# The compressed branch's values in three rounded products instead of one full one

## The reference, cut to what matters

```python
k_cmp = compress(kc.reshape(B, S, G, dh), pe_k, w_ck1, w_ck2)
v_cmp = compress(vc.reshape(B, S, G, dh), pe_v, w_cv1, w_cv2)
...
s_c = jnp.einsum('bqghd,bngd->bghqn', qb, k_cmp) * scale
p_c = masked_softmax(s_c, cmp_end[None, :] <= t[:, None])
o_c = jnp.einsum('bghqn,bngd->bqghd', p_c, v_cmp)
...
o = gb[..., 0:1] * o_c + gb[..., 1:2] * o_s + gb[..., 2:3] * o_w
```

## Time and profile before

| | us |
|---|---|
| three runs | 1516.87, 1518.05, 1518.22 |
| profiled execution: from its first to its last instruction (its whole time isn't listed apart) | 1515.0 |
| TensorE busy | 1499.8 (99%), 7403 matmuls |
| VectorE busy | 895.7 (59%) |
| ScalarE busy | 774.9 (51%) |
| GpSimd busy | 740.0 (49%) |
| the eight full products of the compressed values, 16 records | 8.9 |

### The profile page before, as it was taken

The page is one execution under the profiler, slowest core; times in us unless marked ns, Lnnn a source line. Parts: engine busy times, 40 slices in busy tenths (PEclk is TensorE's granted clock), DMA queues, the critical chain, the costliest instruction groups (busy, mean ns, idle before and its releaser), DMA issues.

```text
span 1515.0 us, 19796 instructions
## 1 busy us (share of the span) xinstructions
PE 1499.8 (99%) x7403; PEld 1185.8 (78%) x7403; DVE 895.7 (59%) x1435; ACT 774.9 (51%) x1237; POOL 740.0 (49%) x462
## 2 busy tenths in 40 slices
PE   9999999999999999999999999999999999999997
PEld 7776657888888888888887787777888888888885
DVE  5568994242235764947545623532102699999998
ACT  6578885223344323132344644632224588888885
POOL 4456675445584745565464664743557362141100
PEclk9999999999999999999999999999999999999999
DMA  9210002322243564555222331121226389999984
GB/s 374 76 51 2 15 15 107 110 91 90 98 139 120 202 222 167 208 188 195 91 90 70 118 118 56 56 84 59 96 99 254 121 344 411 405 394 383 390 336 179
DMA packets 74942, 250.87 MB, mean 166 GB/s; under 512 B 11712, under 2 KB 13056, under 8 KB 74840
## 3 DMA queue, kind: packets, MB, share of 16 engines
q1 hardware_dynamic: 67264, 234.41, 41.9%
q0 software_dynamic: 4752, 8.19, 1.5%
q10 hardware_dynamic: 2824, 6.94, 1.3%
HBM read 244.94 MB, written 12.66 MB: 170 GB/s over the span
## 4 chain that ended last, share of the span: by engine, by line
PE 94%; DVE 4%; ACT 2%; issue 0%; DMA 0%; DVEq 0%; ACTq 0%
PE ps L453 18%; PE ps L457 18%; PE ps L454 18%; PE ps L1118 4%; PE ps L1122 4%; PE ps L1119 4%; PE ps L514 2%; PE ps L1151 2%; PE ps L517 2%; PE ps L1147 2%; PE ps L520 2%; PE ps L1148 2%; PE ps L681 2%; PE ps L715 2%; PE ps L550 2%; PE ps L886 1%
## 5 line engine op out<-in xcount | busy, mean ns | idle before, releaser
L318 POOL TENSOR_TENSOR RS<-RAW,RS 128x1024 fp32r<-128x1024 f32 x172 | 430.2, 2505 | 373.1 <-ACT RS L309 369.5
L309 ACT ACTIVATE RS<-RAW 128x1024 fp32r<-128x1024 f32 x305 | 320.2, 1056 | 227.8 <-PE ps L457 139.2
L453 PE MATMUL ps<-RH,RS 128*128 128x512 f32 x784 | 309.8, 395 | 0.0
L457 PE MATMUL ps<-RH,RS 128*128 128x512 f32 x784 | 305.7, 390 | 0.0
L454 PE MATMUL ps<-RH,RS 128*128 128x512 f32 x784 | 305.6, 390 | 0.0
L453 PEld LDWEIGHTS ps<-RH,RS 128*128 128x128 f32 x784 | 147.3, 188 | 33.9 <-issue 4.1
L457 PEld LDWEIGHTS ps<-RH,RS 128*128 128x128 f32 x784 | 147.2, 188 | 30.9
L454 PEld LDWEIGHTS ps<-RH,RS 128*128 128x128 f32 x784 | 147.3, 188 | 30.7 <-issue 1.0
L318 DVE TENSOR_TENSOR RS<-RAW,RS 128x1024 fp32r<-128x1024 f32 x132 | 155.3, 1221 | 5.9 <-ACT RS L309 5.7
L453 PE MATMUL ps<-RA,RS 128*128 128x512 f32 x400 | 156.7, 392 | 0.0
L454 PE MATMUL ps<-RA,RS 128*128 128x512 f32 x400 | 155.8, 390 | 0.0
(11 more groups left out here) (435 smaller groups left out, 2722.1 us busy)
## 6 DMA issues: line engine op xcount, KB each, us to landing
RAW<-in_w_ff SPq DMA_DIRECT2D x64, 512.0 KB, 4.5
RAW<-in_w_gate SPq DMA_DIRECT2D x45, 512.0 KB, 16.2
RAW<-in_w_up SPq DMA_DIRECT2D x43, 512.0 KB, 17.3
RAW<-in_w_down SPq DMA_DIRECT2D x42, 512.0 KB, 17.3
PB<-in_ada SPq DMA_DIRECT2D x24, 512.0 KB, 3.7
TB<-in_ada SPq DMA_DIRECT2D x24, 512.0 KB, 3.7
RAW<-in_w_gb SPq DMA_DIRECT2D x16, 512.0 KB, 3.2
RAW<-in_w_ga SPq DMA_DIRECT2D x16, 512.0 KB, 3.2
```

The lines of the kernel that those rows point to most:

```text
L309: act.activation(RS[:, spl[n], 0, :], raws[slot[n]], ACT.Copy).then_inc(*HI.up(n))
L318: eng.tensor_tensor(RS[:, s, 1, :], raws[slot[n]], hif(RS[:, s, 0, :]), ALU.subtract).then_inc(*mark.up(n))
L453: pe.matmul(b[:, :], wh, xh, start=(k == 0), stop=False)
L457: last = pe.matmul(b[:, :], wl, xh, start=False, stop=(k == K - 1))
```

## The change

The product of each pair of heads becomes three rounded products into the same buffer. So both factors are made in halves. The new tiles lie in memory where old ones lay: `VBKR` where `VBK` was, `PCR` on `PC`, and the low half of the values on the second half of `TAB` (`TABR`), a table that is read for the last time before.

- The values: the clearing of `VBK` becomes a copy of the cleared `KCZ` to `VBKR`. At 73 us the raw values are also copied to `VRAW`, and `VBKR` takes the rounded values. The low halves are made later (`compressed_values_lo`), in step 1 of the attention: `TABR` is zeroed by a subtraction of ones from ones, then eight subtractions of 31x64 fill its blocks.
- The weights: ScalarE writes the rounded high half in place of the copy (with a wait for the values of step 2 or 6 before it overwrites, for Q of 2 and 3), and VectorE makes the low half out of PSUM (`cmp_back` of `vector`), in step 1 for Q 0, at the end of step 2 for Q 1, and behind the row minima of steps 7 and 12 for Q 2 and 3. It is now VectorE's instruction that frees the PSUM buffer.

```diff
--- before.py
+++ after.py
@@ -181,7 +181,11 @@
     M = sb("M", [128, 8, S])
     PB = sb("PB", [128, 2, 1280])
     TB = sb("TB", [128, 3, 1280])
+    with nc.sbuf_tensor("PCR", [128, 4, S], F32R) as PCR:
+        pass
     PC = sb("PC", [128, 4, S])
+    with nc.sbuf_tensor("TABR", [128, 2, S], F32R) as TABR:
+        pass
     TAB = sb("TAB", [128, 2, S])
     VV = sb("VV", [128, 2, S])
     TMP = sb("TMP", [128, 4, S])
@@ -201,6 +205,8 @@
     RT = sb("RT", [128, 704])
     PE2 = sb("PE2", [128, 32])
     KCZ = sb("KCZ", [128, 4, 32])
+    with nc.sbuf_tensor("VBKR", [128, 4, 128], F32R) as VBKR:
+        pass
     VBK = sb("VBK", [128, 4, 128])
     stat = sb("stat", [128, 3, 4, 4])
     MB = sb("MB", [128, 80], BF16)
@@ -350,6 +356,9 @@
     HID, HTF = TB[:, 1, 0:256], TB[:, 1, 256:512]
     HT = [TB[:, 1, 256:512].rearrange("p (c n) -> p c n", c=2)[:, :, 64 * kv:64 * kv + 62] for kv in range(2)]
     T0, T1 = TB[:, 1, 512:574], TB[:, 1, 576:638]
+    VRAW = TB[0:31, 1, 640:768]
+    VBL = TABR[:, 1, :].rearrange("p (x n) -> p x n", x=4)
+    CPH, CPL = ([PCR[:, 2 * (Q % 2) + x, :] for Q in range(4)] for x in range(2))
     SCQ = [RAW2[:, 3, 0:512], RAW2[:, 3, 512:1024]]
     SCW = [RAW2[:, 7, 0:512], RAW2[:, 7, 512:1024]]
     SCS = [RAW2[:, 2, 128:160], RAW2[:, 2, 160:192]]
@@ -700,10 +709,13 @@
             if br == 0:
                 b = take(("o", pr), (7,))
                 if pr == 0:
-                    pe.wait_ge(*V("vbk"))
-                pe.wait_ge(*A(("ev", ("cb", pr // 2))))
-                pe.matmul(b[:, :], VBK[:, 2 * (pr // 4) + pr % 2, :], PC[:, pr // 2, :], start=True, stop=False,
-                          skip_group_check=True)
+                    pe.wait_ge(*V("vbl"))
+                pe.wait_ge(*V(("ev", ("cb", pr // 2))))
+                vh, vl = (v[:, 2 * (pr // 4) + pr % 2, :] for v in (VBKR, VBL))
+                ph, pl = CPH[pr // 2], CPL[pr // 2]
+                pe.matmul(b[:, :], vh, ph, start=True, stop=False, skip_group_check=True)
+                pe.matmul(b[:, :], vh, pl, start=False, stop=False, skip_group_check=True)
+                pe.matmul(b[:, :], vl, ph, start=False, stop=False, skip_group_check=True)
             if s < 2:
                 pe.wait_ge(*A(("ev", ("vt", 12 + br))))
             b = ps["o", pr]
@@ -1286,7 +1298,10 @@
         def cmp_back(Q):
             if Q == 0:
                 act.wait_ge(*G("masks"))
-            evict(("cb", Q), PC[:, Q, :])
+            elif Q >= 2:
+                act.wait_ge(*P(("npv", 4 * Q - 6)))
+            act.wait_ge(*P(("cb", Q)))
+            act.activation(CPH[Q], ps["cb", Q], ACT.Copy).then_inc(*A.up(("cbh", Q)))
 
         def nsa_weights(n):
             for a in range(2):
@@ -1778,7 +1793,8 @@
                 lo_half(dve, 0, LOV)
         lo_half(dve, 1, LOV)
         dve.memset(KCZ[:, :, :], 0.0).then_inc(*V.up("kcz0"))
-        dve.memset(VBK[:, :, :], 0.0).then_inc(*V.up("vbk0"))
+        after("kcz0")
+        dve.tensor_copy(VBKR[:, :, :], flat(KCZ[:, :, :]).unsqueeze(1).broadcast_to([128, 4, 128])).then_inc(*V.up("vbk0"))
 
 
         def rope_first(u):
@@ -1871,12 +1887,28 @@
             dve.wait_ge(*P(("ck", 0)))
             dve.tensor_copy(T0, ps["ck", 0][:, 0:62]).then_inc(*V.up(("ev", ("ck", 0))))
             dve.wait_ge(*P(("ck", 1)))
+            dve.tensor_copy(VRAW, ps["ck", 1][0:31, 0:128]).then_inc(*V.up("vraw"))
             for g in range(2):
                 for a in range(2):
                     for z in range(2):
                         r0 = 64 * a + 32 * z
-                        dve.tensor_copy(VBK[r0:r0 + 31, 2 * g + a, 64 * z:64 * z + 64],
+                        dve.tensor_copy(VBKR[r0:r0 + 31, 2 * g + a, 64 * z:64 * z + 64],
                                         ps["ck", 1][0:31, 64 * g:64 * g + 64]).then_inc(*V.up("vbk", ("ev", ("ck", 1))))
+
+        def compressed_values_lo():
+            ones4 = onesf[:, :].unsqueeze(1).broadcast_to([128, 4, 128])
+            tt(VBL, ones4, ones4, ALU.subtract, "vbl0")
+            after("vbl0")
+            for g in range(2):
+                for a in range(2):
+                    for z in range(2):
+                        r0 = 64 * a + 32 * z
+                        tt(VBL[r0:r0 + 31, 2 * g + a, 64 * z:64 * z + 64], VRAW[:, 64 * g:64 * g + 64],
+                           hif(VBKR[0:31, 2 * g, 0:64]), ALU.subtract, "vbl")
+
+        def cmp_back(Q):
+            dve.wait_ge(*A(("cbh", Q)))
+            tt(CPL[Q], ps["cb", Q], hif(CPH[Q]), ALU.subtract, ("ev", ("cb", Q)))
 
         def compress_rot():
             dve.wait_ge(*LD["ctb"](0))
@@ -2010,9 +2042,13 @@
             if 0 < n < 16:
                 if n > 1:
                     nsa_shift(n)
+                    if n in (7, 12):
+                        cmp_back({7: 2, 12: 3}[n])
                 else:
                     cmp_soft(1)
                     fin(None)
+                    compressed_values_lo()
+                    cmp_back(0)
                 nsa_weight(n, 0)
                 if n == 1:
                     scaled_gate("w_gb", 0)
@@ -2030,6 +2066,8 @@
                 k = n // 2 - 1
                 out_lo(("o", k), k, A(("oh", k)))
             compressed(15 + n, turn=cmp_turn, soft=cmp_soft)
+            if n == 2:
+                cmp_back(1)
             if n == 17:
                 scaled_gate("w_gb", 2)
```

## The result

| | median, us | lowest to highest | runs |
|---|---|---|---|
| before, beside the first runs of after | 1518.11 | 1516.54 to 1518.24 | 6 |
| after | 1522.43 | 1521.61 to 1523.10 | 6 |
| before, beside the second runs of after | 1516.89 | 1516.47 to 1518.42 | 27 |
| after, second runs | 1523.33 | 1523.01 to 1523.71 | 5 |

The ratio after to before is 1.0034 (95% interval 1.0024 to 1.0045) in the first comparison and 1.0037 (1.0023 to 1.0051) in the second. The first median is 4.3 us up and lies in the predicted range; the forecast was 1522.0. The second pair is 6.4 us apart: something comes on top of the predicted sum that differs from run to run.

The account below looks back on a forecast made before the run. TensorE was taken to bind, in places VectorE and ScalarE. 3.3 - 0.17 + 0.96 - 0.17 - 0.07 + 0.36 - 0.34 + 0.1 = +3.97 us on 1518.05 gave 1522.0, range 1518.3 to 1524.4 (own 1520.9 to 1523.0).

Parts of the forecast that it names:

- The block: Step 1: ten new VectorE instructions (zeros, eight small subtractions, a low half) delay the scores of step 2 by 3.3 us.
- nothing covers this: Step 1: TensorE already waits for VectorE's evictions there, so the whole 3.3 us of new VectorE work delays it.
- Products: Three rounded products save 0.17 us per place, counting only where TensorE sets the pace: one, four, seven and eight.
- rival 2: TensorE's saving counts, waits cover step 1's VectorE work: eight products each end 0.38 us earlier, -3.0, 1515.0; chance 0.12.
- The fifth: Fifth product, at 190.92 us in VectorE's second chain: some 0.07 us of its saving comes through, an estimate.
- First stop: Turning of step 6: TensorE waits until VectorE frees PSUM buffer 2 behind the minima of step 7, +0.96 us.
- Second stop: Turning of step 11: TensorE waits for VectorE's low half in step 12, +0.36 us (bounds 0 and 0.7).
- Second low half: VectorE's 0.61 us ahead of the row minima at 130.17 fits into 1.57 us of idle time, taken at nothing.
- The clearing at 14 us: At 14.14 us, the clearing becomes a copy that waits for the clearing ahead: 0 to +0.3 us, taken as +0.1.
- Sum: All priced gains and losses over the whole kernel together: +3.97 us, giving a median of 1522.0 us.
- the time of start and end: The 3.05 us between the profiled span, 1515.0, and the timed median, 1518.05, taken as time around the span.
- rival 3: VectorE work stretched beside GpSimd's, or clock at 1.2 GHz while TensorE stands: 2 us more, 1524.0; chance 0.11.

## Why the prediction was right, and where not

- **The block** was 3.31 us for the predicted 3.3 (zeros 0.72, eight 1.98, low half 0.61), and the step "nothing covers this" holds: in the kernel before, with the block alone, all 3.31 passed to the end.
- **Products** gave 0.15 to 0.17 each, predicted 0.17; the 0.38 of rival 2 never showed with 128 rows. The fifth was to bring 0.07 and brought nothing that lasted.
- **First stop** +1.02 for +0.96: VectorE's subtraction ended when it was said to, the hand-over to TensorE took 0.15 us (171.58 to 171.73) where 0.05 was taken. **Second stop** +0.58, and less the sixth product's 0.16 +0.42, for +0.36: a hand-over of 0.14 (215.78 to 215.92).
- **Second low half** took nothing: it ran in the wait, with 0.21 us left.
- **The clearing at 14 us** cost nothing (predicted +0.1): the copy starts the next instruction 0.38 us behind itself, the clearing did so in 0.40.
- **Sum** at 300 us, against the base: +4.08 in the first profile of after, +4.10 in the second without its two falls, +4.09 in the one with the stand filled; predicted 3.97.
- **What failed, in a forecast that came out, is the step from the profiled execution to the median.** I called the 3.05 us between the span and the median "the time of start and end". Outside the span there are only 1.8 us (1516.87 - 1515.0 in one execution, 1518.05 - 1516.3 in the other). The other 1.2 came with a fall of the clock, which the second profile of before shows and the first has not. It was in the base unseen.
- **And rival 3's clock was set too low.** The sum put the clock at nothing, and I gave it and other extra losses 0.11, on the ground that the clock was 1.00 over the whole stretch. It was, in a kernel in which TensorE never stood 3 us there. Of four profiles with a stand of 3.2 us, three have the fall behind it. "From 262 us on every stage as long as before" fell with it, near 820 us.

Corrected: 1516.8 us (before with no fall) + 4.1 = 1520.9 with no fall, 1522.4 with one of 1.5 us, 1523.9 with two. The runs of after lie from 1521.6 to 1523.7, so the sum isn't exact for each: the profiled execution with one fall took 1521.61, the one with two 1523.71. The two errors have opposite signs and nearly cancel, so it is in part luck that 1522.0 lies near 1522.43. By the mean granted clock most of after's runs had more than one fall: its first six average 0.9958, the second five 0.9952, against 0.9978 for before with none. Not shown: which falls a single timed run had, since three digits don't tell; why they came more often in the second runs; nor why the first profile of after escaped the one behind the stand.

## What to carry to other kernels

A few small instructions on an engine that frees buffers can cost more than a large product saves: price them at their place, by rows of the same shape and the same partitions, and look for one wide instruction instead (1.2 us for 3.3) or a place behind a wait. A new stand of TensorE can cost more than its length (three of four of 3.2 us did, and one of 2.3); where it couldn't be removed, products of no use in it paid (1.6 us between two profiles). And before a profile's span is set against a median, see that both runs had the same clock.

## What the hardware showed that I had not expected

- Stands of TensorE of 3.24, 3.24, 3.25 and 2.34 us were followed by a stretch at 1.2 GHz of 3.4 us (6.8 once), one of 3.27, two of about 1.15 and one of 0.70 by none. A fall cost 1.4 to 1.6 us, the long one 2.7.
- The same eight 31x64 subtractions took 1.16 us on one group of partitions, 1.95 on four, and 5.14 on four beside GpSimd with both inputs in SBUF; with one input in PSUM, beside GpSimd, 1.94.
- Products with 64 rows in place of 128 took the same 0.23 us among themselves, but the first of them mostly started 0.28 us or less behind a score product of 64 rows (0.05 at the second product), where one with 128 rows took 0.31, and 0.32 behind a product with 128 rows, where one with 128 rows took 0.23.
- In four of twelve profiles, whatever the kernel, the clock fell for 3.4 us near 820 us, behind a stretch of small products.
